# Gated linear attention: diagonal 64x64 squares for six groups of scores, 64-column halves for a head's other native products

## The chip, the cores and the metric

One core of a Trainium2 chip runs the whole program in one launch. The metric is the device time in microseconds of an execution; three runs of the kernel before are shown. Shapes in rows are partitions x elements; "128*64" in a matmul's row is the stationary operand: 128 partitions, 64 columns.

## The reference, cut to what matters

The program is two transformer blocks over 512 tokens of width 1024: a gated delta rule mixer with an MLP, a gated linear attention (GLA) mixer with an MLP, and a block with attention and pooling. The change is in the GLA mixer, four heads with keys of 128 and values of 256, run forwards and backwards over the tokens:

```
def step(state, inp):
    q_c, k_c, v_c, b_c = inp
    dec = jnp.exp(jnp.where(causal, b_c[:, :, :, None, :] - b_c[:, :, None, :, :], -jnp.inf))
    scores = jnp.einsum('bhid,bhjd,bhijd->bhij', q_c, k_c, dec)
    o = jnp.einsum('bhid,bhde->bhie', q_c * jnp.exp(b_c), state) + jnp.einsum('bhij,bhje->bhie', scores, v_c)
    b_last = b_c[:, :, -1:, :]
    state = jnp.exp(b_last[:, :, 0, :])[..., None] * state + jnp.einsum(
        'bhjd,bhje->bhde', k_c * jnp.exp(b_last - b_c), v_c)
    return state, o
```

`b_c` is a cumulative sum of log decays. The kernel works with chunks of 128 tokens (the result of the recurrence does not depend on the size of the chunk).

## The kernel before, in words

The tokens lie in ST = 4 chunks of P = 128. For one head h of the four, scores within a chunk are gathered from eight groups, in the order `SCORES = (None, 1, 2, 3, 4, 0, 5, 6)` (L2470). The group None is k times q without decay, of which only the diagonal is used. Group l (0 to 6) serves the pairs of tokens that lie in the same aligned block of 2*2^l tokens but in different halves of it; for it, q and k are multiplied with decays taken from the middle of that block. So for l from 0 to 5 all pairs that count lie in one of the two diagonal 64x64 squares of the chunk's 128x128 matrix; for l = 6 they lie outside them.

TensorE runs one hand-written order per head, `pe_b_head` (L2522), with these pieces:

- `pe_b_score(h, j)` (L2498): four native fp32 products of 128x128x128, one per chunk (L2510), into PSUM bank 2 or 3. VectorE's `dve_b_merge` (L2688) then puts the entries that count into the tile ST under a mask (L2699; L2695 for the first group) and frees the bank; the score two places later waits for that.
- `pe_b_unit` (L2423): a "unit" makes the cumulative sums of log decays: two single-pass (fp32r) products of width 384 or 512 (L2436, L2437), for r = 8, 9 four transposes (L2443), for r = 10, 11 four fp32r products (L2440, two apiece). ScalarE turns each unit into decays (L2462, L2464). Units use two banks in turn, so a unit waits until ScalarE has read the one two places back. A head has UNITS = 20 of them; the first twelve of the next head are made ahead, four after each of score 6, score 7 and the last state_out.
- `update(cc)` (L2536): key times value for the state, 128x128x256, one for each direction; VectorE adds it to the state (L2711, L2715).
- `state_out(cc)` (L2546): state times decayed query, four products of 128x128x128, accumulated in banks 0 and 1.
- the product of the values with ST (L2580), eight products that close the accumulation, after which come the transposes of the next head's key (L2519, `pe_b_turn`), the next head's score 0, and the sum of squares (`pe_b_out_sum`, L2592), each over the full 128 columns.

The order for heads 0 to 2 is: out_sum of the head before, score 1, 2 units, score 2, 2 units, score 3, 2 units, score 4, 2 units, update 0, score 5, state_out 1, update 1, score 6, 4 units, state_out 2, update 2, score 7, 4 units, state_out 3, 4 units, value times ST, turn, score 0 of the next head. Head 0 has two more units and its turn between score 1 and score 2, and its score 0 stands inside the projection of the values (L2301), between slabs of fp32r products. Head 3 has no units ahead. VectorE's order is `dve_b_head` (L2718): merges, query products (L2686), norms (L2675), decays on queries (L2760), states, and between merges 4 and 5 the split of the next head's log decays (`dve_b_las`, L2408), for which the first unit ahead waits (L2429). Numbers of scores here are places j in SCORES; score 1 is l = 1, score 5 is l = 0, score 6 is l = 5.

In the gated delta stage, early in the same kernel, the products of L1203 and L1224 are already issued as two diagonal 64x64 squares for most levels:

```
for r in square_tiles(h, l):
    n = r.stop - r.start
    at = c % 2 * P + r.start
    mm = nc.tensor.matmul(bk[s][r, at:at + n], a_keys(h)[:, c, r], z_right(h, l, c * P + r.start, n),
                          start=True, stop=True, skip_group_check=True)
```

A native fp32 product stands in the trace as two passes, each with its own weight load and matmul record: four products are "x8".

Of the kernel before, what the change touches and what calls it, by code (L numbers as in the profile page):

```python
# [23 lines left out]
P = 128  # L24
D = 1024
S = 512
ST = S // P
# [4 lines left out]
BDV = 256  # L32
# [4 lines left out]
LEVELS = 7  # L37
# [71 lines left out]
def build(nc, a, out):  # L109

    ctx = ExitStack()
    with ctx:
# [31 lines left out]
        bk = [ctx.enter_context(nc.psum_tensor(f"bk{i}", [P, 512], F32)) for i in range(8)]  # L144
# [20 lines left out]
        def carve(tensor, sizes, start=0):  # L165

            views, at = {}, start
            for name, *shape in sizes:
                n = int(np.prod(shape))
                v = tensor[:, at:at + n]  # L170
                if len(shape) == 2:
                    v = v.rearrange("p (x y) -> p x y", x=shape[0])
                elif len(shape) == 3:
                    v = v.rearrange("p (x y z) -> p x y z", x=shape[0], y=shape[1])
                views[name] = v
                at += n
            assert at <= tensor.shape[1], (at, tensor.shape)
            return views
# [56 lines left out]
        n = 0  # L235
# [4 lines left out]
        n = 0  # L240
# [62 lines left out]
        def mm3(acc, lhs_hi, lhs_lo, rhs_hi, rhs_lo, first, last):  # L303

            nc.tensor.matmul(acc, lhs_hi, rhs_hi, start=first, stop=False, skip_group_check=True)  # L305
            nc.tensor.matmul(acc, lhs_hi, rhs_lo, start=False, stop=False, skip_group_check=True)  # L306
            return nc.tensor.matmul(acc, lhs_lo, rhs_hi, start=False, stop=last, skip_group_check=True)  # L307

        def pe_feature_slab(pe, name, k2, b, width=256, between=None):

            pe.wait_ge(w_ready, k2 * 4 + 2 * (PH[name][0] + b + 1))
            hi, lo = slab_view(whi[b], KT), slab_view(wlo[b], KT)
            for j in range(2):
                if not (isinstance(k2, int) and 2 * FS[name] + 4 * k2 + 2 * b + j < 4):
                    pe.wait_ge(acc_free, k2 * 4 + (2 * FS[name] + 2 * b + j - 3))
                m = min(P, width - j * P)
                c = slice(j * P, j * P + m)
                for kt in range(KT):
                    mm = mm3(bk[2 * b + j][0:m, :], hi[:, kt, c], lo[:, kt, c], act_hi[:, kt, :], act_lo[:, kt, :],
                             kt == 0, kt == KT - 1)  # L320
                mm.then_inc(acc_ready if j == 0 else slab_used, 1)
                if j == 0 and between is not None:
                    between(pe)
# [326 lines left out]
        def sp_token(sp, name):  # L650
            pairs = PH[name][1] // 4
            for half in range(2):
# [3 lines left out]
                else:  # L656
# [25 lines left out]
                    start=9600)  # L682
# [336 lines left out]
        def chunk_of(cc, d):  # L1019
            return cc if d == 0 else ST - 1 - cc  # L1020
# [1168 lines left out]
        def dve_mod(dve, third):  # L2189
# [3 lines left out]
            for i in range(4):  # L2193
# [5 lines left out]
        b_qT = arena[:, 0:2048].rearrange("p (n s) -> p n s", n=BH)  # L2199
        b_kT = arena[:, 2048:4096].rearrange("p (n s) -> p n s", n=BH)  # L2200
        b_v = arena[:, 4096:8192].rearrange("p (c n) -> p c n", c=ST)
# [4 lines left out]
        BB = carve(work, [("masks", 256), ("E", 10 * S), ("ZK0", ST, P), ("ZK1", ST, P), ("ST", ST, P), ("ktok", ST, P),  # L2206
                          ("S0", BDV), ("S1", BDV), ("rs", S), ("gl", 8)], start=4096)
# [10 lines left out]
        def gw3_part(i):  # L2218
            return gw3[:, i, :, :].rearrange("p k (q n) -> p k q n", q=3)

        B = {n: sem("b_" + n) for n in (
            "w2_hi w2_lo gl_lo w_loaded gate_loaded cum_loaded cum_ready masks_loaded masks_ready gate_set w_hi w_ready gl_mm gl la_mm softplus la "
            "las_hi las_lo e_mm exp gl_col zk zq qd kd sc st k_turned k_tok u s o_done o_sq o_sum o_ln o_rs of1 o_out").split()}

        def b_e(d, slot):

            at = E_AT[slot] + (1 - d) * S
            return work[:, at:at + S]

        def b_mix(slot, l, q_side, start=0, width=S):  # L2230

            b, e = 1 << l, work[:, :]
            first = E_AT[slot] + (0 if q_side else S)
            step = S + b if q_side else b - S
            return bass.AP(e.tensor, e.offset + first + start,
                           [list(e.ap[0]), [2 * b, width // (2 * b)], [step, 2], [1, b]])

        def b_slot(l):
            return l - 1 if l > 0 else 8
# [31 lines left out]
        def pe_b_in(pe):  # L2271
# [27 lines left out]
            pe_token_slab(pe, "b_v", 1, 0, 0, 1, True, False, decays_read)  # L2299
            pe.wait_ge(sum_added, 4 * TH["b_v"] + 4)  # L2300
            pe_b_score(pe, 0, 0)  # L2301
            pe_token_slab(pe, "b_v", 1, 0, 1, 1, False, True)

# [194 lines left out]
        def pe_b_score(pe, h, j):  # L2498
            l, n = SCORES[j], 8 * h + j
            if n >= 2:  # L2500
                pe.wait_ge(B["st"], n - 1)
            if l is not None:
                pe.wait_ge(B["zq"], 7 * h + j)
                if l > 0:
                    pe.wait_ge(B["zk"], 6 * h + l)
            for c in range(ST):
                cs = slice(c * P, c * P + P)
                lhs = BB[f"ZK{(6 * h + l - 1) % 2}"][:, c, :] if l else b_kT[:, h, cs]
                rhs = b_qT[:, h, cs] if l is None else b_mix(b_slot(l), l, True, c * P, P)
                mm = nc.tensor.matmul(bk[2 + n % 2][:, cs], lhs, rhs, start=True, stop=True, skip_group_check=True)  # L2510
            mm.then_inc(B["sc"], 1)

        def pe_b_turn(pe, h):
# [8 lines left out]
        def pe_b_head(pe, h):  # L2522
            units = list(range(UNITS * h + (12 if h > 0 else 10), UNITS * h + UNITS))
            ahead = list(range(UNITS * (h + 1), UNITS * (h + 1) + 12)) if h + 1 < BH else []

            def next_units(of, n):
                for _ in range(n):
                    if of:
                        pe_b_unit(pe, of.pop(0))

            def update(cc):
                for d in range(2):
                    c = chunk_of(cc, d)
                    if cc > 0:
                        pe.wait_ge(B["s"], 6 * h + 2 * (cc - 1) + d + 1)
                    nc.tensor.matmul(bk[7 - d][:, 0:BDV], b_e(d, 7)[:, c * P:c * P + P], b_v[:, c, h * BDV:h * BDV + BDV], start=True,  # L2536
                                     stop=True, skip_group_check=True).then_inc(B["u"], 1)

            def state_out(cc):
                for d in range(2):  # L2540
                    c = chunk_of(cc, d)
                    pe.wait_ge(B["s"], 6 * h + 2 * (cc - 1) + d + 1)
                    if cc == 1:
                        pe.wait_ge(B["qd"], 2 * h + d + 1)
                    for e in range(2):
                        nc.tensor.matmul(bk[e][:, c * P:c * P + P], BB[f"S{d}"][:, e * P:e * P + P], b_e(d, 6)[:, c * P:c * P + P],  # L2546
                                         start=cc == 1 and d == 0, stop=False, skip_group_check=True)

            if h == 0:
                pe_b_score(pe, h, 1)  # L2550
                pe.wait_ge(sum_added, 4 * TH["b_v"] + 6)
                next_units(units, 2)
                pe.wait_ge(sum_added, 4 * TH["b_v"] + 8)
                pe_b_turn(pe, h)
                next_units(units, 2)
            for j in range(1 if h > 0 else 2, 5):
                pe_b_score(pe, h, j)
                next_units(units, 2)
            pe.wait_ge(B["kd"], 2 * h + 2)
            if h > 0:  # L2560
                pe.wait_ge(B["o_ln"], h)
            pe.wait_ge(B["k_tok"], h + 1)
            update(0)
            pe_b_score(pe, h, 5)
            if h > 0:
                pe.wait_ge(B["of1"], 2 * h)
            state_out(1)
            update(1)
            pe_b_score(pe, h, 6)
            next_units(ahead, 4)  # L2570
            state_out(2)
            update(2)
            pe_b_score(pe, h, 7)
            next_units(ahead, 4)
            state_out(3)
            next_units(ahead, 4)
            pe.wait_ge(B["st"], 8 * h + 8)
            for c in range(ST):
                for e in range(2):
                    mm = nc.tensor.matmul(bk[e][:, c * P:c * P + P], b_v[:, c, h * BDV + e * P:h * BDV + e * P + P], BB["ST"][:, c, :],  # L2580
                                          start=False, stop=True, skip_group_check=True)
            mm.then_inc(B["o_done"], 1)
            if h + 1 < BH:
                pe_b_turn(pe, h + 1)
                pe_b_score(pe, h + 1, 0)
                pe_b_out_sum(pe, h)
# [1188 lines left out]
```

## Time and profile before

| what | value |
|---|---|
| median of three runs | 1765.11 us (1765.09 to 1765.27) |
| the profiled execution's own time | 1766.39 us |
| its span, first to last instruction | 1764.6 us |
| TensorE (PE) busy | 1731.8 us, 98% |
| VectorE (DVE) busy | 1117.6 us, 63% |
| ScalarE (ACT) busy | 802.4 us, 45% |
| GpSimd (POOL) busy | 280.3 us, 16% |

The profiled execution took 1.28 us more than the median and has 1.8 us around its span. The GLA heads fill 987 to 1096 us of the span. A matmul's record begins when it is taken up and its end is modelled, so records of neighbours overlap; the pace is read from start to start.

### The profile page before, as it was taken

How to read it: one execution, taken by the hardware profiler on the slowest of the kernel's cores; microseconds unless marked ns; L12 is line 12 of the kernel's file. 1: busy time of each engine (PE TensorE's matmuls, PEld its weight loads, DVE VectorE, ACT ScalarE, POOL GpSimd, SP SyncE). 2: the span in 40 equal slices, each digit the busy share in tenths (PEclk: the TensorE clock that was granted, in tenths of full speed). 3: DMA queues.
4: the chain of work that ended last, by engine and by line, in shares of the span. 5: the costliest groups of instructions: out<-in, count | busy, mean ns of one | idle time of the engine just before them, and what ended most of it. 6: DMA issues, size and time to landing. Idle time of an engine off the chain costs nothing.

```text
span 1764.6 us, 26275 instructions
## 1 busy us (share of the span) xinstructions
PE 1731.8 (98%) x10336; PEld 1434.3 (81%) x10336; DVE 1117.6 (63%) x1604; ACT 802.4 (45%) x1352; POOL 280.3 (16%) x268
## 2 busy tenths in 40 slices
PE   8999999999999999999999999999999999999999
PEld 6888777878789988888887878889988888876777
DVE  4776377776788746657421587787746766433763
ACT  4433555554236743333543454246743345434541
POOL 2001175663000010010000253000010010101600
PEclk9999999999999999999999999999999999999999
DMA  5223100000333354332232100333354353430002
GB/s 166 86 88 112 48 14 14 2 1 2 96 96 99 117 166 133 107 127 83 73 95 86 46 13 10 87 98 118 110 178 143 95 168 89 155 96 25 25 1 72
DMA packets 103277, 147.24 MB, mean 83 GB/s; under 512 B 5153, under 2 KB 71153, under 8 KB 102912
## 3 DMA queue, kind: packets, MB, share of 16 engines
q1 hardware_dynamic: 96192, 121.45, 22.0%
q0 software_dynamic: 6976, 24.27, 4.3%
q8 instruction: 76, 1.25, 0.3%
q14 instruction: 33, 0.27, 0.0%
HBM read 143.61 MB, written 2.10 MB: 83 GB/s over the span
## 4 chain that ended last, share of the span: by engine, by line
PE 92%; DVE 4%; issue 1%; ACT 1%; DMA 1%; SPq 0%; DVEq 0%; ACTq 0%
PE bk L307 23%; PE bk L305 23%; PE bk L306 23%; PE bk L1203 2%; PE bk L1224 2%; PE bk L1213 1%; PE bk L3374 1%; PE bk L3375 1%; PE bk L2510 1%; PE bk L3396 1%; PE bk L1240 1%; PE bk L1258 1%; PE bk L1284 1%; PE bk L1249 1%; DMA X<-in_x 1%
## 5 line engine op out<-in xcount | busy, mean ns | idle before, releaser
L284 DVE TENSOR_TENSOR wlo<-raw,whi 128x1024 fp32r<-128x1024 f32 x166 | 198.3, 1232 | 274.1 <-ACT whi L278 273.7
L305 PE MATMUL bk<-act_hi,whi 128*128 128x512 f32 (+1 forms) x880 | 323.8, 368 | 0.3 <-DVE wlo L797 0.3
L307 PE MATMUL bk<-act_hi,wlo 128*128 128x512 f32 (+1 forms) x880 | 320.8, 365 | 0.0
L306 PE MATMUL bk<-act_lo,whi 128*128 128x512 f32 (+1 forms) x880 | 320.8, 365 | 0.0
L305 PE MATMUL bk<-whi,act_hi 128*128 128x512 f32 (+1 forms) x776 | 306.4, 395 | 0.5 <-DVE act_lo L643 0.5
L307 PE MATMUL bk<-whi,act_lo 128*128 128x512 f32 (+1 forms) x776 | 306.8, 395 | 0.0
L306 PE MATMUL bk<-wlo,act_hi 128*128 128x512 f32 (+1 forms) x776 | 304.1, 392 | 0.0
L278 ACT ACTIVATE whi<-raw 128x1024 fp32r<-128x1024 f32 x166 | 168.6, 1054 | 254.9 <-PE bk L307 231.0
L305 PEld LDWEIGHTS bk<-act_hi,whi 128*128 128x128 f32 x880 | 165.7, 188 | 31.2 <-issue 1.1
L306 PEld LDWEIGHTS bk<-act_lo,whi 128*128 128x128 f32 x880 | 165.7, 188 | 29.6 <-issue 1.0
L307 PEld LDWEIGHTS bk<-act_hi,wlo 128*128 128x128 f32 x880 | 165.6, 188 | 29.4
L306 PEld LDWEIGHTS bk<-wlo,act_hi 128*128 128x128 f32 x776 | 145.8, 188 | 35.7 <-issue 0.5
L305 PEld LDWEIGHTS bk<-whi,act_hi 128*128 128x128 f32 x776 | 145.7, 188 | 34.7 <-issue 1.2
L307 PEld LDWEIGHTS bk<-whi,act_lo 128*128 128x128 f32 x776 | 145.7, 188 | 33.4
L305 PE MATMUL bk<-t_ops,whi 128*128 128x256 f32 x320 | 89.5, 280 | 0.0
L306 PE MATMUL bk<-t_ops,whi 128*128 128x256 f32 x320 | 89.5, 280 | 0.0
L307 PE MATMUL bk<-t_ops,wlo 128*128 128x256 f32 x320 | 89.5, 280 | 0.0
L2478 POOL TENSOR_TENSOR work<-work,arena 128x512 f32<-128x512 f32 x24 | 38.2, 1609 | 261.8 <-ACT work L2462 237.4
L518 DVE TENSOR_TENSOR act_lo<-arena,act_hi 128x2048 fp32r<-128x2048 f32 x30 | 68.8, 2293 | 15.6 <-ACT act_hi L512 15.6
L2156 POOL DMA_DIRECT2D work<-in_ln_g x4 | 2.2, 555 | 396.6 <-ACT arena L1991 374.6
L901 DVE SCALAR_TENSOR_TENSOR work<-work,convw 128x512 f32<-128x512 f32 x96 | 64.6, 746 | 0.0
L305 PEld LDWEIGHTS bk<-t_ops,whi 128*128 128x128 f32 x320 | 60.2, 188 | 0.0
(463 smaller groups left out, 3084.7 us busy)
## 6 DMA issues: line engine op xcount, KB each, us to landing
raw<-in_mlp_w SPq DMA_DIRECT2D x100, 512.0 KB, 4.4
raw<-in_a_w_in SPq DMA_DIRECT2D x32, 512.0 KB, 4.0
work<-in_mlp_w SPq DMA_DIRECT2D x28, 512.0 KB, 4.4
work<-in_w_mod POOLq DMA_DIRECT2D x24, 512.0 KB, 3.9
raw<-in_b_w_in SPq DMA_DIRECT2D x24, 512.0 KB, 3.8
raw<-in_w_in SPq DMA_DIRECT2D x14, 512.0 KB, 4.0
raw<-in_a_w_out SPq DMA_DIRECT2D x8, 512.0 KB, 4.0
raw<-in_b_w_out SPq DMA_DIRECT2D x8, 512.0 KB, 4.1
```

The source lines that it names most:

```text
L278: nc.scalar.activation(whi[b][:, hs], src[hf][:, :], ACT.Copy).then_inc(w_hi_ready, 1)
L284: nc.vector.tensor_tensor(wlo[b][:, hs], src[hf][:, :], whi[b][:, hs], ALU.subtract).then_inc(w_ready, 1)
L305: nc.tensor.matmul(acc, lhs_hi, rhs_hi, start=first, stop=False, skip_group_check=True)
L306: nc.tensor.matmul(acc, lhs_hi, rhs_lo, start=False, stop=False, skip_group_check=True)
L307: return nc.tensor.matmul(acc, lhs_lo, rhs_hi, start=False, stop=last, skip_group_check=True)
L518: nc.vector.tensor_tensor(stage(act_lo, b), hid_group(pair, b), stage(act_hi, b), ALU.subtract).then_inc(stage_ready, 1)
L901: nc.vector.scalar_tensor_tensor(out=acc, in0=src, scalar=wk, in1=acc, op0=ALU.mult, op1=ALU.add).then_inc(conv_step, 1)
L1203: mm = nc.tensor.matmul(bk[s][r, at:at + n], a_keys(h)[:, c, r], z_right(h, l, c * P + r.start, n), start=True, stop=True, skip_group_chec ...
L1213: mm = nc.tensor.transpose(bk[(2, 4)[s]][:, c % 2 * P:c % 2 * P + P], A["MB"][:, c, :], eye[:, :])
L1224: mm = nc.tensor.matmul(level_sum(l, s)[r, at:at + r.stop - r.start], A["X"][:, c, r], A["T"][:, c, r], start=True, stop=True, skip_group_ ...
L1240: nc.tensor.matmul(scan_read(d), A[f"ke{d}"][:, chunk_of(cc, d), :], A["S"][:, 2 * d + cc % 2, :], start=True, stop=True, skip_group_check ...
L2478: nc.gpsimd.tensor_tensor(halves(out, l), b_mix(b_slot(l), l, False), halves(b_kT[:, h, :], l), ALU.mult).then_inc(B["zk"], 1)
```

## The change

The scores of six groups (l = 0 to 5) are issued per chunk as two products, each with 64 columns of the stationary key and the 64 query columns of the same square. Score 0 (None), score 7 (l = 6), update, state_out and the value product go through a new helper that issues each product as two, each with 64 columns of the stationary operand and the whole moving operand. Units, transposes and out_sum stay as they are.

```
+        def mm_halves(acc, lhs, rhs, first, last):
+
+            for r in (slice(0, P // 2), slice(P // 2, P)):
+                mm = nc.tensor.matmul(acc[r, :], lhs[:, r], rhs, start=first, stop=last, skip_group_check=True)
+            return mm
...
                 lhs = BB[f"ZK{(6 * h + l - 1) % 2}"][:, c, :] if l else b_kT[:, h, cs]
-                rhs = b_qT[:, h, cs] if l is None else b_mix(b_slot(l), l, True, c * P, P)
-                mm = nc.tensor.matmul(bk[2 + n % 2][:, cs], lhs, rhs, start=True, stop=True, skip_group_check=True)
+                if l is None or l == LEVELS - 1:
+                    rhs = b_qT[:, h, cs] if l is None else b_mix(b_slot(l), l, True, c * P, P)
+                    mm = mm_halves(bk[2 + n % 2][:, cs], lhs, rhs, True, True)
+                    continue
+                for q in range(2):
+                    rows, at = slice(64 * q, 64 * q + 64), c * P + 64 * q
+                    mm = nc.tensor.matmul(bk[2 + n % 2][rows, at:at + 64], lhs[:, rows], b_mix(b_slot(l), l, True, at, 64),
+                                          start=True, stop=True, skip_group_check=True)
...
-                    nc.tensor.matmul(bk[7 - d][:, 0:BDV], b_e(d, 7)[:, c * P:c * P + P], b_v[:, c, h * BDV:h * BDV + BDV], start=True,
-                                     stop=True, skip_group_check=True).then_inc(B["u"], 1)
+                    mm_halves(bk[7 - d][:, 0:BDV], b_e(d, 7)[:, c * P:c * P + P], b_v[:, c, h * BDV:h * BDV + BDV], True, True
+                              ).then_inc(B["u"], 1)
...
-                        nc.tensor.matmul(bk[e][:, c * P:c * P + P], BB[f"S{d}"][:, e * P:e * P + P], b_e(d, 6)[:, c * P:c * P + P],
-                                         start=cc == 1 and d == 0, stop=False, skip_group_check=True)
+                        mm_halves(bk[e][:, c * P:c * P + P], BB[f"S{d}"][:, e * P:e * P + P], b_e(d, 6)[:, c * P:c * P + P],
+                                  cc == 1 and d == 0, False)
...
-                    mm = nc.tensor.matmul(bk[e][:, c * P:c * P + P], b_v[:, c, h * BDV + e * P:h * BDV + e * P + P], BB["ST"][:, c, :],
-                                          start=False, stop=True, skip_group_check=True)
+                    mm = mm_halves(bk[e][:, c * P:c * P + P], b_v[:, c, h * BDV + e * P:h * BDV + e * P + P], BB["ST"][:, c, :],
+                                   False, True)
```

## Rows read from the trace of the kernel before

**Rows 1.** The page: the span, busy time of the engines, and the granted clock in slices.
```profile
span 1764.6 us, 26275 instructions
PE 1731.8 (98%) x10336; PEld 1434.3 (81%) x10336; DVE 1117.6 (63%) x1604; ACT 802.4 (45%) x1352; POOL 280.3 (16%) x268
...
PEclk9999999999999999999999999999999999999999
```

**Rows 2.** Busy time in the stretch from the first score to the last head's end.
```profile
974.00:1097.00 123.00, 118.69 (x718) 99.71 (x717) 91.29 (x119) 59.40 (x115) 44.35 (x28) 1.00 0.06 18
```

**Rows 3.** Critical chain, head 1 into head 2: start us, us, what.
```profile
1013.87 0.89 PE bk L2510 x8
...
1016.49 0.97 PE bk L2510 x8
...
1017.48 0.75 DVE work L2699
...
1029.78 0.61 ACT work L2462
...
1036.67 0.89 PE bk L2546 x8
1037.56 0.45 PE bk L2443 x4
...
1039.96 1.78 PE bk L2580 x16
1041.75 0.44 PE bk L2519 x4
1042.18 0.89 PE bk L2510 x8
1043.08 1.72 PE bk L2592 x4
```

**Rows 4.** Timeline of VectorE in heads 0 and 1: start us, us, idle before.
```profile
991.31 0.75 DVE L2699 COPY_PREDICATED work<-work,bk 128x512 f32<-128x512 uint8 x1 [1.21 <-PE bk L2510]
...
1017.48 0.75 DVE L2699 COPY_PREDICATED work<-work,bk 128x512 f32<-128x512 uint8 x1 [0.54 <-PE bk L2510]
...
1027.63 1.21 DVE L2408 TENSOR_TENSOR b_las<-arena,b_las 128x1024 fp32r<-128x1024 f32 x1
```

**Rows 5.** Timeline of TensorE: first unit ahead in head 1, and head 3's end.
```profile
1028.99 0.47 PE L2436 MATMUL bk<-b_cum,b_las 128*128 128x512 f32 x1
...
1088.56 1.16 PE L2546 MATMUL bk<-work 128*128 128x128 f32 x8 [0.29 <-DVE work L2715]
```

**Rows 6.** Timeline of TensorE in the gated delta stage: squares between full products.
```profile
270.04 0.69 PE L1224 MATMUL bk<-work 128*64 128x64 f32 x16
270.66 0.71 PE L1240 MATMUL bk<-work 128*128 128x128 f32 x4
271.21 0.61 PE L1249 MATMUL bk<-work 128*128 128x128 f32 x4
271.65 0.61 PE L1258 MATMUL bk<-work,arena 128*128 128x128 f32 x4
272.10 1.06 PE L1158 MATMUL bk<-arena,work 128*128 128x128 f32 x8
273.09 0.69 PE L1203 MATMUL bk<-work 128*64 128x64 f32 x16
273.70 0.66 PE L1213 MATMUL bk<-eye,work 128*128 128x128 f32 x4
274.20 0.61 PE L1284 MATMUL bk<-work 128*128 128x128 f32 x4
```

**Rows 7.** Line 1203, source view: ns shortest/median/longest, first and last start, forms.
```profile
L1203 PE MATMUL bk<-work x344: 222/222/377, 206.1 to 396.0; 128*64 128x64 f32 x152, 128*128 128x128 f32 x20
```

**Rows 8.** Groups by line and shape: busy us, mean ns, idle before.
```profile
L2510 PE MATMUL bk<-work 128*128 128x128 f32 x192 | 26.1, 279 | 0.4
...
L2510 PE MATMUL bk<-work,arena 128*128 128x128 f32 x32 | 6.2, 342 | 0.0
```

## The prediction, made before the result was known

> **What bounds the kernel now.** I read the page first: TensorE is busy 98% of the span and its granted clock stands at the upper level, 2.4 GHz, in every slice [rows 1]. Then the busy time of the stretch that the change touches: of 123 us TensorE is busy 118.69 and VectorE 91.29 [rows 2]. That looks like a TensorE bound, but the chain of waits splits each head in two. Score 1 of a head ends at 1017.46, and VectorE takes over at 1017.48; the chain comes back to TensorE's and ScalarE's alternation only with the units ahead, near 1029.78 [rows 3]. The timeline of VectorE says why: it is idle 0.54 us before the merge of score 1, waiting for TensorE, and from there it works without a pause to the end of the split of the log decays at 1027.63 + 1.21 = 1028.84, for which the first unit ahead waits (it starts at 1028.99) [rows 4, 5]. So between score 1 and the units ahead some 11 us per head belong to VectorE, and what TensorE gains or loses in scores 2 to 6, update 0 and 1 and state_out 1 is covered. In the second part (units ahead, state_out 2, update 2, score 7, state_out 3, value times ST, turn, score 0, out_sum, score 1) the chain runs through TensorE and through ScalarE's reading of units that TensorE has just made [rows 3]: time there counts in full.
>
> **What a square costs.** The gated delta stage has both forms side by side. A block of four full products (x8) starts its successor 0.89 us later [rows 3], 0.11 us a pass, and so do x4 blocks: 271.21 to 271.65 is 0.44 [rows 6]. A block of eight squares (x16) starts its successor 0.61 to 0.62 us later [rows 6]. Its 16 records fit in a row of 0.69 us, against 1.06 us for x8 full ones, so two squares run beside each other, at some 0.06 us for a pass of both where a full pass takes 0.11.
>
> **What changing between the forms costs.** Into squares: from 272.10 to 273.09 the full x8 block takes 0.99 instead of 0.89, so the first square starts 0.10 late. Its own slot is about 0.05 longer: the row is 0.69 long and one record 0.22 [rows 7], so the last square starts 0.47 after the first, and seven slots of 0.06 make 0.42. I take 0.15 for an entry. Out of squares: the block's 0.62 holds 0.10 that isn't a slot, and the full block after it takes 0.55 (270.66 to 271.21) where the next takes 0.44: 0.20 for an exit to full products. Out into transposes (273.70 to 274.20 is 0.50, rows of 0.66 against 0.61) it is 0.10 + 0.05 = 0.15. All from [rows 6]. An isolated block of squares is thus worth 0.89 - 0.10 - 0.62 - 0.11, some 0.06 us; but its last result is there at 0.10 + 0.69 = 0.79 instead of 1.06, that is 0.27 earlier. Trainium skill, TensorEngine Tiling (Array Packing), "Key Properties": changing the tiling mode, unlike changing the tile, drains the engine. The rows agree, with 0.10 us of it on either side.
>
> **Halves.** No row shows 64 stationary columns with 128 or 256 moving ones. Lower bound: a pair in the time of one square pair, 0.06 a pass; but the full pass of 128 moving columns takes 0.11 and the square's of 64 takes 0.06, so the time goes with the moving columns and a half streams all 128. Upper bound: no overlap, two times 0.11. The nearest row is the squares', whose two tiles do overlap; I take 0.11 for the pair, as for one full product. So halves gain nothing by themselves, and only keep the engine in the form of the squares where squares are neighbours. They are that only in update 0 to score 6. Everywhere else units, transposes or out_sum stand between, and the halves bring entries and exits where there were none.
>
> **The sum, on the path.** In each of the three passages from a head to the next:
> - state_out 2, update 2, score 7, between units: 0.15 + 0.20 = +0.35
> - state_out 3, between a unit and the transposes of L2443: 0.15 + 0.15 = +0.30
> - value times ST, between a unit and the turn: +0.30
> - score 0, between the turn and out_sum: +0.35
> - score 1, squares after out_sum: its end, for which VectorE waits, -0.27; VectorE's 0.54 us of idling leaves room for it [rows 4].
>
> That is +1.03, three times +3.09. Score 0 of head 0 stands between fp32r slabs: +0.35. In head 0 VectorE begins its unbroken run after score 2 (idle 1.21 before 991.31) [rows 4], so score 1 with its exit and score 2 count: -0.27 + 0.20 - 0.27 = -0.34. Head 3 has no units ahead, stays in the new form from update 0 to the value product and waits for VectorE at 1088.56 [rows 5]; only the exit after the value product counts, +0.20. Sum: 3.09 + 0.35 - 0.34 + 0.20 = **+3.3 us**.
>
> **What I cost at nothing.** Scores 2 to 6, update 0 and 1, state_out 1: hidden under VectorE's run. Without that cover, scores 2 to 4 would save 0.06 each, and update 0 to score 6 would pay one entry and exit, 0.35, against two blocks of squares that save 8 x 0.05 = 0.4 each. The exit from score 6 falls into the wait for L2408 (score 6 is over before 1028.84 either way). Score 5 (l = 0) takes 342 ns a record against 279 [rows 8], since its moving operand is read element by element from two places; as squares it may gain anything from nothing to half, hidden in both cases. The added matmuls (one more for each of 232 products) add no DMA and no semaphore. GpSimd's key products start from ScalarE's copy of the turned key, not from the scores, except for waits that lie well before them. The entry and exit could be off by 0.03 each (rows are rounded to 0.01 and I add two or three readings); 33 of them count (9 in each passage, 6 elsewhere), so 1.0 us.
>
> **Rivals.**
> - **A: TensorE's time counts everywhere.** For it: 98% busy. Against: VectorE's run without a pause. Then each head below 3 gets score 0 +0.35, scores 1 to 4 -0.06 each, update 0 to score 6 0.35 - 0.8 = -0.45, and +0.35 + 0.30 + 0.30: +0.6; head 3 gets 0.35 - 0.24 - 0.45 = -0.3. Sum +1.5; score 5's four blocks are busy for 6.2 us, 1.55 each against 26.1 / 24 = 1.09 [rows 8]; if squares halve that too, it is a further 4 x 0.23 less: +0.6 to +1.5 us, 1765.7 to 1766.6.
> - **B: it becomes faster, because the switch isn't paid.** The blocks of squares in the gated delta stage each wait for a result of another engine; if the 0.10 is that wait and no price of the form, halves and units here follow each other without a gap, and only score 1 (three heads) and scores 1 and 2 of head 0 remain, at 8 x 0.05 = 0.4 each: -2.0 us, 1763.1. It decides if entries and exits on the path cost under 0.03 us each. Against it: the same 0.10 on each side after four different lines in [rows 6].
> - **C: halves don't overlap fully.** A passage has 48 narrow passes (score 0, state_out 2 and 3, score 7: 8 each; value product: 16) and 4 wide ones on the path. With no overlap: 48 x 0.11 + 4 x 0.21 = 6.1, three times 18.4, and 0.9 and 2.6 for score 0 of head 0 and the end of head 3: +22 on top of 3.3, 1790. With the matmuls beside each other but each pass's weights not loaded behind the one before, up to 0.06 a pass: 52 x 0.06 x 3 + 0.5 + 1.4 = 11, with 3.3: 1780. The Trainium skill, TensorE: Matmul & The Clock Gate, "Part 3: Packing small matmuls", says that weight loads overlap running matmuls only when the row group differs; here it is the same for both halves. By that rule it would be 1780. The squares speak against it: 16 loads and 16 matmuls of one row group in 0.69 us.
> - **D: the squares of this stage gain nothing** (read patterns of the mixed decays): score 1 becomes later, not earlier; 5 x 0.4 = 2.0 more, 1770.4.
>
> **The numbers.** Main case 0.72, A 0.12, B 0.05, C 0.07, D 0.04. Against the profiled execution's 1766.39 us the sum gives 1769.7; that one stands 1.3 us above the median, so the forecast on the runs is 1765.11 + 3.3 = 1768.4. A measurement can tell about 0.2%, 3.5 us, from no change; the forecast is just inside. The main case reaches from +2.3 to +4.3 with the entries and exits, and I give a little over a third of it to above 3.5. Slower: 0.27 + C 0.07 + D 0.04 = 0.38. Faster: B and a little, 0.06. Same: 0.56. The range goes from A's upper part to D: 1765.4 to 1770.6, leaving out B, C and the bottom of A.
>
> **What would show it.** Right: in the timeline, squares' blocks of x16 some 0.5 to 0.6 us to the next start; halves' rows of x16 with 0.9 us to the next start plus 0.10; first units after score 7 with a record 0.1 longer; VectorE's idle before the merge of score 1 down to about 0.3 relative to its other work; a head's period up from 28.3 us (1013.87 to 1042.18, [rows 3]) to about 29.3; the chain still through VectorE between score 1 and the units ahead. Wrong: a period unchanged or shorter (A or B), halves' blocks of 1.8 us (C), VectorE's run broken by waits for TensorE, or a granted clock below the upper level in the stretch.

## The result, and the profile after

| | before | after |
|---|---|---|
| median | 1766.39 us (20 runs) | 1768.79 us (20 runs) |
| ratio | | 1.0015, 95% interval 1.0008 to 1.0021 |
| span of the profiled execution | 1764.6 us | 1768.8 us |
| stretch: start of head 0's score 0 to the first fp32r product after head 3's value product | 116.50 us | 118.72 us |
| period: score 0 of head 1 to score 0 of head 2 | 28.31 us | 29.04 us |

The change costs 0.0015 x 1766.4, that is 2.6 us (1.4 to 3.7): within 0.2% of no change, as forecast. One of the twenty executions after took 2714 us, at a lower clock, and is left out of the ratio, as are single ones of 2420 and 4333 us among the runs of the experiments. The medians of one group of runs and another differ by a microsecond for the same kernel (1765.11 of three runs, 1766.39 of twenty), so stretch and period, which are read inside one execution and lie within the change's reach, tell the small differences better. The two spans differ by 4.2 us, but of that 0.6 lies ahead of the stretch and 1.3 behind it, where the kernels are the same.

The page after, against [rows 1]:

```profile
span 1768.8 us, 27203 instructions
PE 1733.3 (98%) x10800; PEld 1422.2 (80%) x10800; DVE 1116.3 (63%) x1604; ACT 802.6 (45%) x1352; POOL 280.0 (16%) x268
...
PEclk9999999999999999999999999999999999999999
```

464 more matmul records (two for each of 232 added products), and a clock at the upper level throughout. In the stretch, though, TensorE is busy less. Its busy time is the first number after the length, before and after:

```profile
974.90:1091.40 116.50, 112.19 (x693) 95.06 (x692) 89.36 (x117) 56.50 (x109) 44.35 (x28) 1.00 0.06 19
...
975.50:1094.20 118.70, 110.68 (x1157) 80.32 (x1156) 88.13 (x117) 56.48 (x109) 44.28 (x28) 1.00 0.06 19
```

TensorE was busy 112.19 us of 116.50 and is busy 110.68 of 118.70: 1.5 us less work and 3.7 us more idle time. The timeline of TensorE in head 1 shows the pieces; most gaps are too short to be listed as idle time and are read from start to start. Columns: start, length, line, shape, records; lines behind 307 have moved (2510 is now 2521 for squares, and 312 for what goes through the helper; 2592 is 2604).

```profile
1030.26 0.47 PE L2442 MATMUL bk<-b_cum,b_las 128*128 128x512 f32 x1 [0.49 <-DVE b_las L2414]
...
1032.85 1.09 PE L312 MATMUL bk<-work 128*64 128x128 f32 x16
1033.77 1.03 PE L312 MATMUL bk<-arena,work 128*64 128x256 f32 x8
1034.64 1.04 PE L312 MATMUL bk<-work 128*64 128x128 f32 x16
1035.61 0.50 PE L2442 MATMUL bk<-b_cum,b_las 128*128 128x512 f32 x1
...
1038.18 1.09 PE L312 MATMUL bk<-work 128*64 128x128 f32 x16
1039.20 1.09 PE L2449 MATMUL bk<-eye,arena 128*128 128x128 f32 x8
...
1041.76 1.97 PE L312 MATMUL bk<-work,arena 128*64 128x128 f32 x32
1043.66 0.66 PE L2531 MATMUL bk<-eye,arena 128*128 128x128 f32 x4
1044.24 1.09 PE L312 MATMUL bk<-arena 128*64 128x128 f32 x16
1045.27 1.98 PE L2604 MATMUL bk<-act_f,ones 128*128 128x512 f32 x4
1047.18 0.72 PE L2521 MATMUL bk<-work 128*64 128x64 f32 x16
1047.83 0.44 PE L2442 MATMUL bk<-b_cum,b_las 128*128 128x384 f32 x1
```

Score 0 as halves takes 1.03 us to the next start (1044.24 to 1045.27), where the x8 block of full products took 0.89 [rows 3]. Score 1 as squares takes 0.65. Inside one form no price is seen: update 2 to score 7 is 0.87, where full products took 0.86, and state_out 2 to update 2, right behind an entry, is 0.92 for 0.89. The pieces of the period, start to start in the two timelines:

| piece of head 1 into head 2 | before | after | difference |
|---|---|---|---|
| first unit ahead to state_out 2 | 2.50 | 2.59 | +0.09 |
| state_out 2, update 2, score 7 | 2.56 | 2.76 | +0.20 |
| units to state_out 3 | 2.46 | 2.57 | +0.11 |
| state_out 3 to transposes (L2443/2449) | 0.89 | 1.02 | +0.13 |
| to the value product | 2.40 | 2.56 | +0.16 |
| value product to turn | 1.78 | 1.90 | +0.12 |
| turn to score 0 | 0.44 | 0.58 | +0.14 |
| score 0 to out_sum | 0.89 | 1.03 | +0.14 |
| out_sum to score 1 | 1.72 | 1.91 | +0.19 |
| score 1 to VectorE's merge of it | 1.17 | 0.77 | -0.40 |
| that merge to the first unit ahead | 11.51 | 11.35 | -0.16 |
| sum | 28.32 | 29.04 | +0.72 |

The chain of waits goes to VectorE after score 1 and comes back with the units ahead, as I had read it in [rows 3]:

```profile
1018.21 0.68 PE bk L2521 x16
1018.91 0.75 DVE work L2711
...
1028.90 1.22 DVE b_las L2414
1030.26 0.47 PE bk L2442
1031.05 0.61 ACT work L2468
```

In the kernel before, the profile's chain comes back earlier, with state_out 1, update 1 and score 6, which my reading left out:

```profile
1026.18 0.68 PE bk L2546 x4
1026.86 0.87 PE bk L2536 x4
1027.72 0.09 issue
1027.81 1.13 PE bk L2510 x8
1028.94 0.05 issue
1028.99 0.47 PE bk L2436
```

The two paths end together there: VectorE's split ends at 1028.84 and score 6, by its modelled end, at 1028.94. The first unit ahead starts 0.15 after the split's end in both kernels (1028.84 to 1028.99, 1030.11 to 1030.26), which speaks for VectorE as what held it. After the change it is clear: TensorE is idle 0.49 us before that unit and waits for L2414.

And the timelines of VectorE and of GpSimd in head 1, against [rows 4]:

```profile
1018.91 0.75 DVE L2711 COPY_PREDICATED work<-work,bk 128x512 f32<-128x512 uint8 x1 [0.72 <-PE bk L2521]
1019.56 1.57 DVE L2698 TENSOR_TENSOR work<-work,arena 128x512 f32<-128x512 f32 x1
...
1025.51 0.76 DVE L2723 COPY work<-bk 128x256 f32<-128x256 f32 x2
...
1028.90 1.21 DVE L2414 TENSOR_TENSOR b_las<-arena,b_las 128x1024 fp32r<-128x1024 f32 x1
...
1019.30 2.98 POOL L2484 TENSOR_TENSOR work<-work,arena 128x512 f32<-128x512 f32 x2
```

VectorE's idle time before the merge of score 1 is 0.72 instead of 0.54, not the 0.3 that I named. From the merge of score 0 to that of score 1 it is 2.57 us instead of 2.68, so 0.11 less; but the query product between them takes 1.25 instead of 1.53, since it starts 0.57 behind GpSimd's state key (1016.95 and 1016.38) where it started 0.29 behind it (1015.41 and 1015.12). What VectorE saves there it spends waiting. L2723, the copy that reads update 0, shows no wait: VectorE's run is unbroken.

### The profile page after: what moved, and what is told of

It reads as the page before. It is cut to its first block, busy times and chain, and to the rows that moved or that the text cites. A ratio compares the mean times of both kernels' runs of the same rounds, so it can differ in the third digit from the quotient of the medians.

```text
span 1768.8 us, 27203 instructions
## 1 busy us (share of the span) xinstructions
PE 1733.3 (98%) x10800; PEld 1422.2 (80%) x10800; DVE 1116.3 (63%) x1604; ACT 802.6 (45%) x1352; POOL 280.0 (16%) x268
## 4 chain that ended last, share of the span: by engine, by line
PE 91%; DVE 5%; issue 2%; ACT 1%; DMA 1%; SPq 0%; DVEq 0%; ACTq 0%
PE bk L307 23%; PE bk L305 23%; PE bk L306 23%; PE bk L1209 2%; PE bk L1230 2%; PE bk L1219 1%; PE bk L312 1%; PE bk L3386 1%; PE bk L3387 1%; PE bk L3408 1%; PE bk L1246 1%; PE bk L1264 1%; PE bk L1290 1%; PE bk L1255 1%; DVE work L2711 1%
```

## The experiments

Stretch and period are defined above; intervals are 95%, against the kernel before on the same chip. "Theory R" and "theory S" in the expectations are two readings of why the squares' gain is lost, first stated for e5.

| run | ratio | interval | stretch | period |
|---|---|---|---|---|
| before | | | 116.50 | 28.31 |
| the change | 1.0015 | 1.0008 to 1.0021 | 118.72 | 29.04 |
| e1 squares only | 0.9995 | 0.9986 to 1.0004 | 116.05 | 28.30 |
| e2 squares in score 1 (and 2 of head 0) | 1.0004 | 0.9995 to 1.0013 | 116.87 | 28.53 |
| e3 halves only | 1.0042 | 1.0028 to 1.0056 | 123.91 | 30.24 |
| e4 squares, halves only between scores 4 and 6 | 0.9999 | 0.9990 to 1.0008 | 116.07 | 28.30 |
| e5 the change, score 0 whole | 1.0011 | 1.0001 to 1.0020 | 118.33 | 29.00 |
| e6 squares, update 0 before score 4 | 1.0015 | 1.0006 to 1.0024 | 119.38 | 28.63 |
| e7 the same order without squares | 1.0017 | 1.0008 to 1.0026 | 119.55 | 28.57 |
| e8 the same order with the change | 1.0031 | 1.0020 to 1.0042 | 121.74 | 29.37 |
| e9b squares, update 0 before the last units | 0.9988 | 0.9979 to 0.9997 | 114.68 | 27.82 |
| e10b the same order without squares | 1.0009 | 1.0000 to 1.0018 | 118.15 | 28.85 |
| e11b as e9b, out_sum behind score 1 | 0.9988 | 0.9979 to 0.9997 | 114.86 | 27.90 |

**e1, squares without halves.** Against the kernel before:

```
+                if l is None or l == LEVELS - 1:
                     (rhs and the matmul as before)
+                    continue
+                for q in range(2):
+                    rows, at = slice(64 * q, 64 * q + 64), c * P + 64 * q
+                    mm = nc.tensor.matmul(bk[2 + n % 2][rows, at:at + 64], lhs[:, rows], b_mix(b_slot(l), l, True, at, 64), ...)
```

> Squares for the six groups, every other product whole as before. The stretch is counted from the first record of head 0's score 0 to the first fp32r product after head 3's value product: 116.5 us before, 118.7 after the change; a head's period (score 0 of head 1 to score 0 of head 2) is 28.3 before and 29.0 after. My theory (only what stands after the units ahead and before the end of score 1 counts; the run of VectorE hides scores 2 to 6): every entry and exit on the path is gone but that into score 1, score 1 ends 0.27 to 0.30 sooner, period about 28.0, stretch 115.3, time 1.2 us below before. Rival A (TensorE's time counts everywhere): scores 1 to 4 save 0.06 each and scores 5 and 6 0.1 to 0.3 each, period 27.8 to 28.0, stretch 114.7 to 115.5: the same size, told apart by the next run. Rival D (squares gain nothing): 116.5 or more.

Neither: the period did not fall at all. Head 0's part of the stretch (score 0 to score 0 of head 1) did fall, by 0.36 (38.44 for 38.80), the 0.34 that the prediction gave its scores 1 and 2; in head 0 GpSimd has no state keys. The timelines of VectorE and GpSimd in head 1 say why the others gained nothing:

```profile
1015.69 0.76 DVE L2705 COPY_PREDICATED work<-work,bk 128x512 f32<-128x512 uint8 x1 [0.25 <-PE bk L2515]
1016.34 0.80 DVE L2692 TENSOR_TENSOR work<-work,arena 128x512 f32<-128x512 f32 x1
...
1020.93 0.66 DVE L2766 TENSOR_TENSOR work<-work,arena 128x512 f32<-128x512 f32 x1
1022.49 0.86 DVE L2717 COPY work<-bk 128x256 f32<-128x256 f32 x2 [0.90 <-PE bk L2542]
...
1016.54 3.75 POOL L2478 TENSOR_TENSOR work<-work,arena 128x512 f32<-128x512 f32 x2
```

and TensorE's:

```profile
1020.44 0.69 PE L2515 MATMUL bk<-work 128*64 128x64 f32 x16 [0.41 <-POOL work L2478]
```

The same query product and keys in the kernel before:

```profile
1018.12 1.77 DVE L2686 TENSOR_TENSOR work<-work,arena 128x512 f32<-128x512 f32 x1
...
1018.05 2.98 POOL L2478 TENSOR_TENSOR work<-work,arena 128x512 f32<-128x512 f32 x2
```

Score 1 did end 0.3 sooner (VectorE's idle time before its merge fell from 0.54 to 0.25). But now VectorE's query product starts 0.20 before GpSimd's key product (1016.34 and 1016.54); in the kernel before it started 0.07 after it. I call this the race. The query product takes 0.80 instead of 1.77, and GpSimd's two keys take 3.75 instead of 2.98. Score 4 waits for the second key, update 0 stands behind score 4 in TensorE's order, and VectorE waits 0.90 us for update 0. A wait that the trace of before doesn't show takes the place of what the squares gained: from the merge of score 1 to the first unit ahead it is 11.77 us (1015.69 to 1027.46) instead of 11.51.

**e2, squares only where I held them to be on the path.** The edit of e1 with the condition `not (j == 1 or (h, j) == (0, 2))` for the full form.

> Squares for score 1 of each head and score 2 of head 0 alone, all else as before. My theory: these are the only squares on the path, so the same stretch as with all six groups, 115.3 us, and a period of 28.0. Rival A: 5 blocks at 0.06, 116.2 us, period 28.25.

The period rose by 0.2 instead, and the stretch is 0.8 longer than with all six groups. The race is lost in the same way (query product 0.80, keys 3.74 in its trace), and now score 4, which waits for GpSimd's key, is a full block of 0.89 where e1 has 0.62; VectorE waits 1.16 for update 0 instead of 0.90. So squares beyond score 1 do count here, by that second chain: my theory that nothing in scores 2 to 6 matters is wrong once GpSimd's chain is the longer one. Rival A's 28.25 missed too, by less than my 28.0.

**e3, halves everywhere.** In the changed kernel the condition for halves in `pe_b_score` is `True`.

> All that the change touches as halves, no squares at all. My theory: four excursions a passage at 1.2 us together, score 1 ends 0.15 later instead of 0.3 sooner, so the period is 28.3 + 1.3 = 29.6 to 29.8 and the stretch 121 to 123 (the run of VectorE may be broken by scores 2 to 4, each 0.35 dearer). If halves by themselves saved time beside the switch (their weights load in half the time), the period would stay under 29.3. Rival A: scores 1 to 4 add 0.35 each in place of -0.06, period 29.0 + 4 x 0.4 + 2 x 0.4 = 31.4.

Period 30.24, above the 29.8 of my theory and well below rival A's 31.4; stretch 123.91. Scores 2 to 4 now reach beyond VectorE's cover (TensorE runs without a gap from score 1 to update 1 in the chain, and VectorE waits 0.62 for update 0). Its stretch is above the 121 to 123 too. I see no gain of the halves' own beside the switch: the x16 blocks of scores 2 to 4 take 1.02 to 1.03 to the next start, in the other form, 0.89 plus what the change of form adds inside the block.

**e4, halves only in update 0, state_out 1 and update 1.** The changed kernel, with the other callers of the helper issuing one matmul.

> Squares for the six groups, halves only in update 0, state_out 1 and update 1, which stand between scores 4 and 6; score 0, score 7, state_out 2 and 3, update 2 and the value product whole. My theory: halves there are under VectorE's run and cost and save nothing: stretch and period as with squares only (115.3 and 28.0). Rival A: one entry and exit instead of two or three there, 0.3 to 0.6 a head less than squares only.

The same as squares only to 0.02 us, in period and stretch, and rival A's 0.3 to 0.6 a head did not come. But it is no clean test of the cover. GpSimd is behind here as in e1, so update 0 is on the path: VectorE waits 1.06 for it instead of 0.90 (the entry makes it later), and its next decay product takes 1.07 instead of 1.23, which gives the 0.16 back. The absolute values missed as in e1.

**e5, the changed kernel with score 0 whole.**

> The changed kernel with score 0 alone whole again. Squares alone gave no gain (period 28.30, as before), and their trace shows why: VectorE's query product L2686/L2692 now starts 0.2 us before GpSimd's key product L2478 instead of 0.07 after it; of two that overlap, the one that starts first takes 0.8 (VectorE) or 1.27 (GpSimd), the other waits out the first and takes 1.77 or 1.74 to 2.05. So GpSimd's two keys take 3.75 instead of 2.98, score 4 waits for them, update 0 stands behind score 4, and VectorE idles 0.9 us before L2711. In the changed kernel GpSimd is 0.26 us ahead. Theory R (that race): with score 0 whole the merge of score 1 comes 0.28 to 0.34 sooner against GpSimd, VectorE gets ahead, the keys take over 3.5, and the period does not fall: 29.0 to 29.3. Theory S (prices add up, no race): the period falls by an entry and an exit, 29.04 to 28.7.

29.00: theory R, and not the 28.7 of theory S. An entry and an exit fewer (0.33 by the table above) brought 0.04. In its trace VectorE is ahead, and the wait is there:

```profile
1016.96 0.68 DVE L2702 TENSOR_TENSOR work<-work,arena 128x512 f32<-128x512 f32 x1
...
1023.15 0.86 DVE L2727 COPY work<-bk 128x256 f32<-128x256 f32 x2 [1.06 <-PE bk L316]
...
1017.05 3.75 POOL L2488 TENSOR_TENSOR work<-work,arena 128x512 f32<-128x512 f32 x2
```

0.09 us between two starts (1016.96 and 1017.05) decide over 0.77 us of GpSimd's time, and the keys take 3.75 as in e1.

**e6, e7, e8: update 0 ahead of score 4**, with squares only, in the kernel before, and in the changed kernel:

```
             for j in range(1 if h > 0 else 2, 5):
+                if j == 4:
+                    (the waits for kd, o_ln and k_tok)
+                    update(0)
                 pe_b_score(pe, h, j)
                 next_units(units, 2)
```

> Squares only, and update 0 put ahead of score 4, so that VectorE's states do not wait behind GpSimd's key for score 4. Theory R: VectorE's 0.9 us of idling before the state copy goes, and score 1's gain counts: period 27.4 to 27.7, stretch 113.5 to 114.5, time 2 us or more below before. Theory S (the squares' gain is lost otherwise): period stays at 28.3.

> The control: the kernel before with update 0 ahead of score 4, no squares. Theory R: in the kernel before GpSimd wins the race by 0.07 us and VectorE never waits for update 0, so nothing changes: period 28.3, stretch 116.5, unless the race flips by chance, when it still does not delay the states. If it gains as much as the run with squares, the order and not the squares is what pays there.

> The changed kernel with update 0 ahead of score 4. Two more changes of form (entry before update 0, none saved), under VectorE's run. Theory R: GpSimd is ahead in the changed kernel and VectorE's run is unbroken there, so nothing is gained: period 29.0 to 29.1.

All three are slower than what they start from, and all three missed: 28.63, 28.57 and 29.37. In e6 the wait for update 0 is gone, but with update 0 ahead of score 4 the last two units come later, and VectorE waits for the decays that ScalarE copies from them (L2638 in the kernel before, L2645 here):

```profile
1024.07 0.74 DVE L2718 COPY work<-bk 128x256 f32<-128x256 f32 x2
1025.78 1.62 DVE L2767 TENSOR_TENSOR work<-work,arena 128x512 f32<-128x512 f32 x1 [0.97 <-ACT work L2645]
```

In e7 and e8 head 1 has no such wait; their second decay product grows from 1.10 and 1.12 to 1.36 and 1.44, as it now meets GpSimd's next keys (in e7 these start at 1025.66 and it at 1026.13). In head 0 of e6 the move costs over 2 us (its part of the stretch is 40.68 against 38.44 in e1), since update 0 waits 1.19 for state keys that VectorE makes late there. So e6 doesn't tell the theories apart; I had looked at what waits for update 0 and not at what was queued behind it.

**e9b, e10b: update 0 before the last two units**, in heads 1 to 3, with squares only and in the kernel before:

```
+                if j == 4 and h > 0:
+                    (the waits for kd, o_ln and k_tok)
+                    update(0)
+                    next_units(units, 2)
                 pe_b_score(pe, h, j)
                 next_units(units, 2)
```

> Squares only; in heads 1 to 3 update 0 after the units behind score 3, then the last two units, then score 4; head 0 in the old order. The last try at this put update 0 and score 4 ahead of the last units, so that L2638, which reads their decays, came late and VectorE waited 0.97 us for it before the second decay product; in head 0 TensorE waited for VectorE's state keys. Here the last units keep their place. Theory R (what eats the squares' gain is VectorE's wait for update 0 behind score 4 behind GpSimd's key): the idle 0.9 us before L2711 falls to 0.0 to 0.4, period 27.4 to 27.9, stretch 114.5 to 115.5, time 1 us or more below before. Theory S: period 28.3.

> The control: the same order without squares. Theory R: GpSimd wins the race by 0.07 us in the kernel before and VectorE's run has no gap, so this order has nothing to give: period 28.2 to 28.4, stretch 116.3 to 116.7. If VectorE gets ahead by chance, keys grow to over 3.5 us as with squares, and the period still does not rise, since nothing waits for them: 27.9 to 28.4.

With squares: period 27.82, stretch 114.68, ratio 0.9988. The gap before the state copies is gone, while GpSimd still loses the race:

```profile
1021.69 0.67 DVE L2771 TENSOR_TENSOR work<-work,arena 128x512 f32<-128x512 f32 x1
1022.27 0.75 DVE L2722 COPY work<-bk 128x256 f32<-128x256 f32 x2
...
1017.31 3.75 POOL L2478 TENSOR_TENSOR work<-work,arena 128x512 f32<-128x512 f32 x2
```

With the wait removed and the race as in e1, the period is 0.48 below e1's: the wait for update 0 behind GpSimd's keys is what ate the squares' gain. Against the kernel before it is 0.49: the 0.30 of score 1, and 0.20 by which VectorE's run is shorter (11.31 from the merge of score 1, 1016.45, to the first unit ahead, 1027.76, for 11.51).

The control missed: 28.85 instead of 28.2 to 28.4. There GpSimd keeps the first race, but the last units are done earlier, GpSimd's next keys start at 1022.66, 0.11 before VectorE's first decay product at 1022.77, and that one takes 1.71 instead of 0.65. The same pair in the control and in the kernel before:

```profile
1022.77 1.71 DVE L2765 TENSOR_TENSOR work<-work,arena 128x512 f32<-128x512 f32 x1
...
1022.66 2.96 POOL L2478 TENSOR_TENSOR work<-work,arena 128x512 f32<-128x512 f32 x2 [2.52 <-ACT work L2462]
```

```profile
1023.68 0.65 DVE L2760 TENSOR_TENSOR work<-work,arena 128x512 f32<-128x512 f32 x1
...
1023.63 3.53 POOL L2478 TENSOR_TENSOR work<-work,arena 128x512 f32<-128x512 f32 x2 [2.60 <-ACT work L2462]
```

In the kernel before the two records start 0.05 us apart, and it is GpSimd that pays there.

The order by itself loses 0.5 us a head and the squares by themselves gain nothing; together they gain 0.5 a head.

**e11b, e9b with out_sum moved behind score 1.**

```
                 pe_b_score(pe, h, j)
+                if j == 1:
+                    pe_b_out_sum(pe, h - 1)
...
                 pe_b_score(pe, h + 1, 0)
-                pe_b_out_sum(pe, h)
```

> The kernel of the run e9b with the sum of squares (out_sum, L2592, 1.7 us of TensorE) moved behind score 1 of the next head. VectorE idles only 0.25 us before the merge of score 1 with squares, so by theory R at most 0.25 a head: period 27.2 to 27.9. The norms L2675 need out_sum's result through ScalarE 4.7 us after score 1; it comes 0.6 later than before, so no new wait there.

27.90, nothing gained. VectorE no longer idles before the merge of score 1, but its next query product meets GpSimd for longer (1.15 instead of 0.81), the next merge starts 1.84 after that of score 1 instead of 1.53, and the second decay product waits 0.22 for ScalarE.

The version that beats both kernels with one more edit than the squares is e9b: 0.9988 of the time before (0.9979 to 0.9997), about 2 us. e11b has the same ratio, with a further edit.

## Why the prediction was right, point by point

**The bound.** Right for the changed kernel: from the end of score 1 to the first unit ahead the chain is VectorE's, which has no wait in its run. What TensorE saved there became idle time before the first unit ahead (0.49 us, where the trace of before lists none), which answers rival A. My reading of the kernel before was a little too sure: its chain passes through state_out 1, update 1 and score 6 on TensorE, 0.1 us from VectorE's path. That scores 2 to 6 can't matter holds in the changed kernel, but only because GpSimd's keys come in time. I looked at VectorE's run for gaps and not at how near the next chain was: turn, ScalarE's copy, two state keys, two keys, score 4, update 0. In e1, e2 and e5 it is the longer one.

**Price of a square block and of halves.** Right. Squares took 0.62 us to the next start (0.65 for score 1), and halves the time of a full block. From score 2 to score 3 to score 4, two units between each, the steps are 1.51 and 1.52 us instead of 1.59: an isolated block gains 0.07 to 0.08 (forecast 0.06). Score 5, left open between nothing and half, took 0.90 to the next start instead of 1.41. Rival C and the rule of the Trainium skill cited there, that weight loads overlap running matmuls only in another row group, are excluded for this case: 16 records with their 16 weight loads fit into 1.03 us, change of form included, and state_out 2 takes 0.92 to the next start, where eight full ones took 0.89. Rival D is excluded by the squares' 0.62 to 0.65, and rival B by the table: no block escapes its 0.09 to 0.14 at the entry.

**Entries and exits.** Right in kind, a little too dear. Read from the table, with each next block's late start counted to the exit: state_out 2 to score 7 cost 0.30 (forecast 0.35), state_out 3 0.30 (0.30), the value product 0.25 (0.30), score 0 0.33 (0.35): 1.18 against 1.30.

**Score 1.** -0.30 (the table's -0.40 and its entry of 0.10) against -0.27.

**The term that was missed.** VectorE's run after the merge of score 1 became 0.16 us shorter, where I had it unchanged. The query product after that merge took 1.57 instead of 1.77: it starts 0.26 behind GpSimd's key instead of 0.07 behind it, and so waits less for it. I had priced GpSimd at nothing, by asking only when its products start and not what they do to VectorE's. Passage by passage the forecast was +1.03 and the period gave +0.73: 0.16 from VectorE's run, 0.12 from the four excursions, 0.03 from score 1.

**The sum.** Forecast for the stretch +3.3, measured +2.2: the part of head 0 (score 0 to score 0 of head 1) +0.85, heads 1 and 2 +0.73 and +0.75, head 3 to the end -0.10. Head 3's was forecast at +0.28 (0.35 - 0.27 for its scores 0 and 1, +0.20 at the end); from its score 0 to the merge of its score 1 it gained 0.06, then 0.14 in VectorE's run, and its exit cost 0.10. In the runs' time it is +2.6 (1.4 to 3.7). So the range and "same" before "slower" held; the reason for which it held, more changes of form than gain on the path, is the one given.

**What was right by luck.** That 1768.4 lies so near the measured 1768.79 is luck: the kernel before measured 1.3 us more with the result than in the three runs that I added to, and the medians lie 2.4 us apart instead of my 3.3. That squares gain 0.27 at score 1 is true in the changed kernel only because its other edits, dear as they are, delay score 1 enough to leave GpSimd ahead (by 0.26): without those of score 0 the race is lost (e5). Had the halves been left out, the same step of the sum would have been wrong by its whole size (e1: 28.30 instead of 28.0).

## What to carry to other kernels

Price a change of TensorE's form by the blocks around it: here an excursion from full products into 64-column ones and back cost 0.25 to 0.33 us, so a block of eight squares pays only just when it stands alone (0.07 to 0.08), and by these prices keeping its neighbours in halves pays only where that removes a change; no run had such a case on the path. When an engine's run covers a piece of another engine's work, look for the second longest chain into that run as well, here GpSimd's, before costing a gain ahead of it at its full size; and before moving a step, list what was queued behind it.

## What the runs showed of the hardware that I had not expected

When VectorE and GpSimd each ran a 128x512 product of two SBUF operands at the same time, they did not share: the one that started first about kept its time, the other waited it out. Four traces show it for the same pair of instructions, the query product after the merge of score 1 and GpSimd's first key: VectorE first by 0.20 (e1) or 0.09 (e5) takes 0.80 or 0.68; behind by 0.07 or 0.26 (before, the change) it takes 1.77 or 1.57. GpSimd's two keys take 3.75 in the first two and 2.98 in the others. The Trainium skill says in SBUF — State Buffer, "Who interferes with whom", that a VectorE instruction with two SBUF inputs contends with a GpSimd instruction that reads SBUF, and that "Issue order, not op shape, decides who blocks". The traces agree, with these numbers. The starts in the records tell the order only down to about 0.1 us: the decay product 0.05 behind GpSimd in the kernel before took 0.65, 0.11 behind it in e10b 1.71. From before to e5 the two starts moved by 0.16 us against each other (0.07 behind to 0.09 ahead), and GpSimd's keys took 0.77 us more, so small edits upstream gave results of either sign.
